# Rotary position exchange by two half-partition copies instead of a matrix product, in a two-block transformer kernel on one core

## The chip, the cores and the metric

The kernel runs on one core of one Trainium2 chip. The metric is the device time of one execution in microseconds (us); lower is better. The core has TensorE (PE, matrix products), VectorE (DVE), ScalarE (ACT), GpSimd (POOL) and the DMA queues; each engine works off its own instructions in order and waits on semaphores.

## What is computed

Two transformer blocks run one after the other on 256 rows of width 1024, all in float32. The first block (conditioned norms, a gated feed-forward, a mixed attention, another feed-forward) has no rotary positions. The second has two layers, and both rotate their queries and keys. Cut to what matters:

```python
def apply_rope(x, cos, sin):                  # x: (B, S, heads, 64), half = 32
    half = x.shape[-1] // 2
    x1, x2 = x[..., :half], x[..., half:]
    return jnp.concatenate([x1 * c - x2 * s, x2 * c + x1 * s], axis=-1)

# layer 1, differential attention: 8 heads, two score maps of 64 dims each
q, k, v = jnp.split(hn @ w_qkv, [1024, 2048], axis=-1)
q = apply_rope(q.reshape(B, S, 16, 64)); k = apply_rope(k.reshape(B, S, 16, 64))
p = softmax(causal(q k^T / 8)); a = p[:, :, 0] - lam * p[:, :, 1]
o = rms_norm(a @ v, subln_g) * (1 - lambda_init); h = h + o @ w_o
h = h + sq_relu_mlp(rms_norm(h))
# layer 2, latent attention: 8 heads, scores over 128 plain + 64 rotated dims
ckv = rms_norm(h) @ w_dkv; c, k_rope = ckv[..., :256], apply_rope(ckv[..., 256:])
q = rms_norm(hn @ w_dq) @ w_uq                # per head 128 plain + 64 rotated
s = (q_nope k_nope^T + apply_rope(q_rope) k_rope^T) * 192**-0.5
h = h + (softmax(causal(s)) @ v) @ w_o; h = h + sq_relu_mlp(rms_norm(h))
return rms_norm(h, final_norm_g)
```

## The kernel before

All weights come through one stream of 1 MB chunks into a ring of five (`raw`); each chunk holds two units of 128x1024. `feed()` splits a unit into a high part (ACT, line 358, `whi`) and the remainder (DVE, line 359, `wlo`), again in a ring of five, and every product of weights is three matmuls (high by high, low by high, high by low: `products`, line 396). Activations are held transposed, features on the 128 partitions and the 256 rows along the free dimension. Small products go through `put` (line 406) and `put_last` (line 409) in plain float32.

PSUM is handed out as a queue of banks (`banks.take`, `banks.give`): four, and four more (`fix`) while they aren't needed as accumulators. A bank that is given back carries the tokens that its next user must wait for. The engines' instructions are emitted in one program order by hand, and the attention heads are threaded into it: a head is a generator (`diff_head`, `latent_head`), and `side.nudge()` advances at most two waiting pieces each time that it is called; a piece names after how many nudges it wants to be continued.

**Layer 1.** For each head `hh`, a q block and a k block of 128 columns are projected (`block_T`, 24 matmuls of 128x256, one nudge in the middle and one behind `feed()`). Each block is then rotated by `roped`. The columns of a block are two heads' halves in their natural order (x1, x2 of one, x1, x2 of the other, 32 partitions each), so the exchange of x1 and x2 is a product with a 128x128 signed permutation, `rotm`:

- ACT copies the block from its bank into `xb` (line 1411, tile `sg`); POOL multiplies it by cosines into `yb` (line 1412, tile `hm`). Here the generator yields.
- At the next nudge, in the middle of the next block (`rope_end`, put in front of the queue by `side.soon`), PE multiplies `xb` by `rotm` into the other half of the bank (line 409), DVE multiplies that by sines (line 1416), gives the bank back, and adds `yb`: one add for k (line 1420), two adds of 64 partitions for q (line 1422), which go into `padded`, where each of the two score maps has its own 128-partition tile with zeros in the other map's half.

A `diff_head` has four pieces: masks, scores, maxima (DVE, line 1153), exponentials (ACT, line 1158) and scaling (DVE, lines 1461 to 1469); the transposes of the probabilities (PE, line 1131; ACT, line 1134); the product with v, the sum of squares (ACT, line 1479), the root by `rstd` (DVE, line 529, then a power on POOL, line 523) and the scaling (DVE, line 1483); the transposes back and the split (PE, line 1490; ACT, line 580; DVE, line 581).

**Layer 2.** One block gives the rotated key `kr`, whose second half of `roped` is called one block of `ukn` later; then `UQ_ORDER` takes for each of four groups one rotated block and two plain ones (`qn`, lines 1642 and 1644). The second half of `roped` is called behind the next plain block's copy. `latent_head` is the head here: scores, exponentials, scaling (DVE, line 1605), then transposes and product with v.

After the loop of each layer `banks.retire(fix)` takes the four accumulator banks out, from the last head's q block in layer 1 and from the third block before the end in layer 2, since the output projection needs them.

Of the kernel before, what the change touches and what calls it, by code (L numbers as in the profile page):

```python
# [7 lines left out]
P = 128  # L8
D = 1024
T = 256  # L10
# [35 lines left out]
for _name, _n in (("ident", 128), ("ones", 128), ("rot", 128), ("tri", 128), ("causal", 128), ("strict", 128), ("flip", 128),  # L46
                  ("cos", 256), ("sin", 256), ("topk", 512), ("bucket", 384)):
    CONST[_name] = (_at, _at + _n)
    _at += _n
# [178 lines left out]
def build(nc, stream, x, c_row, cols, const, g_post, rel, lam, final_g, out):  # L228
    plan = stream_plan()
    with ExitStack() as ctx:  # L230
# [283 lines left out]
        lohi = (slice(0, 64), slice(64, 128))  # L514
        t_zero = t_half
        for c in range(2):
            t_zero = pool.do(lambda e: e.memset(padded[lohi[1 - c], c:24:2, :], 0.0), t_zero)

        def power(r, v, t):
# [3 lines left out]
            return pool.do(lambda e: e.tensor_tensor(r, v, ex, ALU.pow), t, t_zero)  # L523
# [863 lines left out]
        gate_load(2, dve.last(), pe.last())  # L1387
        def other_gates():
            while todo:
                modulations(True)  # L1390
# [13 lines left out]
        cos, sin, rotm = const_of("cos"), const_of("sin"), const_of("rot")  # L1404
        xs = Rooms([Room(sg[:, n, :]) for n in range(2)])
        ys = Rooms([Room(hm[:, n, :]) for n in range(2)])

        def roped(o, b, tk, s):

            xb, yb = xs.take(), ys.take()  # L1410
            t = act.do(lambda e: e.activation(xb.ap, b.ap[:, 0:T], ACT.Copy, scale=s), tk, xb.free)
            t0 = pool.do(lambda e: e.tensor_tensor(yb.ap, xb.ap, cos, ALU.mult), t, yb.free)
            yield
            tk = put_last(b.ap[:, T:2 * T], rotm, xb.ap, True, t)
            turned = o if o.shape[1] == T else xb.ap
            t = dve.do(lambda e: e.tensor_tensor(turned, b.ap[:, T:2 * T], sin, ALU.mult), tk,  # L1416
                       [] if turned is o else t0)
            banks.give(b, t)
            if turned is o:
                t = [dve.do(lambda e: e.tensor_tensor(o, o, yb.ap, ALU.add), t, t0)]  # L1420
            else:
                t = [dve.do(lambda e: e.tensor_tensor(o[q, c, :], xb.ap[q, :], yb.ap[q, :], ALU.add), t, t0)
                     for c, q in enumerate(lohi)]
            xs.give(xb, *t)
            ys.give(yb, *t)
            yield t
# [72 lines left out]
        def rope_end(at, rope):  # L1499
            t_q[at], born[at] = next(rope), side.now  # L1500
            yield

# [302 lines left out]
```

How the kernel before makes its waits and increments, by code:

```python
    def wait(self, *after):  # L116
        for a in after:
            for sem, value in ([a] if isinstance(a, tuple) else a or []):
                if self.seen.get(id(sem), 0) < value:
                    self.seen[id(sem)] = value
                    self.engine.wait_ge(sem, value)
# [1 line left out]
    def do(self, op, *after):  # L124
        self.wait(*after)
        self.count += 1
        op(self.engine).then_inc(self.sem, 1)
        return self.sem, self.count
# [6 lines left out]
    def load(self, out, in_, sem, value, *after):  # L136
        self.wait(*after)
        self.engine.dma_start(out, in_).then_inc(sem, 16)
        return sem, value
```

## Time and profile before

| | |
|---|---|
| median of 3 runs | 1213.88 us (1212.95 to 1217.24) |
| the profiled execution | 1212.7 us |
| its span, first to last instruction | 1211.4 us |
| mean granted TensorE clock | 0.988 |
| PE busy | 1151.8 us (95%), 7570 instructions |
| DVE busy | 808.5 us (67%) |
| ACT busy | 622.6 us (51%) |
| POOL busy | 54.7 us (5%) |

The span is what the trace covers; the execution is 1.3 us longer. The layer-1 blocks with their heads lie at about 617 to 704 us of the span and the layer-2 blocks with theirs at 939 to 1002 us. A busy time is the union of an engine's instructions; matmuls overlap each other in the records, so what one costs is read from the chain, where consecutive starts are shown.

### The profile page before, as it was taken

The page shows a single profiled execution, that of the slowest core. Times are in us where ns is not written, and L with a number is a line of the kernel's source. Part 1 is how long each engine was busy: PE and PEld are TensorE (multiplying, and loading weights), DVE is VectorE, ACT ScalarE, POOL GpSimd, SP SyncE. Part 2 cuts the span into 40 slices and gives each one's busy share as a digit, 9 for nine tenths or more (in the row PEclk, how much of TensorE's full clock was granted, in tenths as well). Part 3 has the DMA queues.
Part 4 walks back from the last instruction along what each step waited for, and adds up shares of the span by engine and source line. Part 5 has one row for each costly group of instructions (what it writes and reads, how often), then busy time and mean ns, then how long its engine had stood idle before and what let it go on. Part 6 is the DMA issues. An engine that isn't in the chain of part 4 may idle for free.

```text
span 1211.4 us, 19269 instructions
## 1 busy us (share of the span) xinstructions
PE 1151.8 (95%) x7570; PEld 1052.6 (87%) x7570; DVE 808.5 (67%) x1334; ACT 622.6 (51%) x1138; POOL 54.7 (5%) x75
## 2 busy tenths in 40 slices
PE   4999999899998999999999898999999889999998
PEld 4988899699987999999799778999998778899997
DVE  4878888777666756555768767565558666656555
ACT  5644444646656544444644455544556444554453
POOL 3100000000001000000012100000000100000000
PEclk9999999999999899999999899999999999999999
DMA  8969998373222566655352234555554413555540
GB/s 345 407 260 411 341 351 308 139 298 118 105 105 71 200 239 211 227 198 176 128 190 100 95 105 150 198 176 195 186 180 153 154 63 102 212 199 177 195 150 35
DMA packets 34009, 231.75 MB, mean 191 GB/s; under 512 B 3704, under 2 KB 5120, under 8 KB 6528
## 3 DMA queue, kind: packets, MB, share of 16 engines
q1 hardware_dynamic: 31952, 226.24, 51.2%
q10 hardware_dynamic: 1968, 4.29, 1.0%
q8 instruction: 60, 0.98, 0.3%
q14 instruction: 29, 0.24, 0.1%
HBM read 229.45 MB, written 1.06 MB: 190 GB/s over the span
## 4 chain that ended last, share of the span: by engine, by line
PE 77%; DVE 11%; ACT 8%; issue 2%; DMA 1%; POOL 1%; DVEq 0%; SPq 0%; ACTq 0%; POOLq 0%
PE ps L396 35%; PE pacc L396 34%; DVE wlo L359 4%; ACT whi L358 2%; PE ps L406 2%; PE ps L409 2%; ACT wk L1158 2%; PE pacc L406 1%; ACT arena L669 1%; POOL st L523 1%; DVE st L1153 1%; DVE tmp L711 1%; DMA raw<-in_stream 1%; DMA cst<-in_const 1%; PE pacc L409 1%
## 5 line engine op out<-in xcount | busy, mean ns | idle before, releaser
L359 DVE TENSOR_TENSOR wlo<-raw,whi 128x1024 fp32r<-128x1024 f32 x353 | 430.2, 1225 | 177.1 <-ACT whi L358 168.7
L358 ACT ACTIVATE whi<-raw 128x1024 fp32r<-128x1024 f32 x353 | 368.8, 1055 | 163.1 <-PE pacc L396 83.2
L396 PE MATMUL ps<-nhi,whi 128*128 128x256 f32 x1256 | 362.7, 289 | 2.6 <-DVE arena L1416 1.1
L396 PE MATMUL ps<-nlo,whi 128*128 128x256 f32 x1256 | 357.0, 284 | 0.0
L396 PE MATMUL ps<-nhi,wlo 128*128 128x256 f32 x1256 | 356.9, 284 | 0.0
L396 PEld LDWEIGHTS ps<-nhi,whi 128*128 128x128 f32 x1256 | 242.4, 193 | 8.5 <-DVE arena L1416 1.4
L396 PEld LDWEIGHTS ps<-nlo,whi 128*128 128x128 f32 x1256 | 242.4, 193 | 4.4 <-issue 0.5
L396 PEld LDWEIGHTS ps<-nhi,wlo 128*128 128x128 f32 x1256 | 242.3, 193 | 0.0
L879 ACT ACTIVATE sg<-ps 128x256 f32<-128x256 f32 x104 | 39.9, 384 | 165.2 <-PE ps L396 165.2
L396 PE MATMUL pacc<-whi,mhi 128*128 128x512 f32 x240 | 95.6, 398 | 0.0
L396 PE MATMUL pacc<-wlo,mhi 128*128 128x512 f32 x240 | 94.0, 392 | 0.0
L396 PE MATMUL pacc<-whi,mlo 128*128 128x512 f32 x240 | 93.5, 390 | 0.0
L881 DVE TENSOR_TENSOR hm<-sg,ps 128x256 f32<-128x256 f32 x104 | 43.6, 420 | 69.8 <-ACT sg L879 69.8
L336 DVE SCALAR_TENSOR_TENSOR raw<-raw,silu_c 128x1024 f32<-128x1024 f32 x72 | 87.6, 1225 | 0.0
L396 PE MATMUL pacc<-whi,hhi 128*128 128x512 f32 x188 | 74.1, 394 | 3.9 <-DVE hlo L888 3.2
L396 PE MATMUL pacc<-wlo,hhi 128*128 128x512 f32 x188 | 73.6, 391 | 0.0
L396 PE MATMUL pacc<-whi,hlo 128*128 128x512 f32 x188 | 73.2, 389 | 0.0
L523 POOL TENSOR_TENSOR st<-st,mod 128x1 f32<-128x1 f32 (+1 forms) x40 | 24.9, 623 | 1006.6 <-DVE st L674 801.6
L396 PE MATMUL pacc<-whi,nhi 128*128 128x512 f32 (+1 forms) x128 | 50.8, 397 | 7.4 <-DVE nlo L750 3.8
L396 PEld LDWEIGHTS pacc<-whi,mlo 128*128 128x128 f32 x240 | 45.1, 188 | 9.9
L396 PEld LDWEIGHTS pacc<-whi,mhi 128*128 128x128 f32 x240 | 45.3, 189 | 8.2 <-issue 0.5
L396 PEld LDWEIGHTS pacc<-wlo,mhi 128*128 128x128 f32 x240 | 45.3, 189 | 7.7 <-issue 0.5
(316 smaller groups left out, 1783.3 us busy)
## 6 DMA issues: line engine op xcount, KB each, us to landing
raw<-in_stream SPq DMA_DIRECT2D x213, 1024.0 KB, 4.9
gates<-in_g_post ACTq DMA_DIRECT2D x3, 512.0 KB, 7.4
h<-in_x SPq DMA_DIRECT2D x1, 1024.0 KB, 7.2
cst<-in_const ACTq DMA_DIRECT2D x1, 1024.0 KB, 4.8
arena<-bias_rows ACTq DMA_DIRECT2D x1, 1024.0 KB, 14.4
out<-tmp SPq DMA_DIRECT2D x4, 256.0 KB, 2.2
silu_c<-in_c_row ACTq DMA_DIRECT2D x1, 512.0 KB, 5.8
arena<-in_final_g SPq DMA_DIRECT2D x1, 512.0 KB, 3.8
```

The lines of the kernel that those rows point to most:

```text
L336: t = dve.do(lambda e: e.scalar_tensor_tensor(src, src, 1.0, silu_c[:, :], ALU.mult, ALU.mult, accum_out=adac[:, 8 * m + k:8 * m + k + 1]) ...
L358: t_hi = act.do(lambda e: e.activation(whi[:, s, :], src, ACT.Copy), arrived, room)
L359: t_lo = dve.do(lambda e: e.tensor_tensor(wlo[:, s, :], src, whi[:, s, :].bitcast(F32), ALU.subtract), arrived, room, t_hi)
L396: return e.matmul(o, lt[a], rh[b], start=start and first, stop=stop and last)
L406: pe.quiet(lambda e: e.matmul(o, lt, rh, start=start, stop=stop), *after)
L409: return pe.do(lambda e: e.matmul(o, lt, rh, start=start, stop=True), *after)
L523: return pool.do(lambda e: e.tensor_tensor(r, v, ex, ALU.pow), t, t_zero)
L669: return act.do(lambda e: e.activation(junk, src, ACT.Square, scale=D ** -0.5, accum_out=sums[:, f:f + 1]), *after)
L711: t = dve.do(lambda e: e.tensor_scalar(tmp[:, i, w], h[:, i, w], r, None, ALU.mult), t, self.new[i])
L879: t = act.do(lambda e: e.activation(sg[:, m, :], up if gate is None else gate, ACT.Relu if gate is None else ACT.Silu), tk)
L881: t = dve.do(lambda e: e.tensor_tensor(hm[:, m, :], sg[:, m, :], up, ALU.mult), t)
L1158: toks.append(act.do(lambda e: e.activation(dst.ap[:, a:a + w], src[:, a:a + w], ACT.Exp, bias=mx[:, i:i + 1], accum_out=sm[:, i:i + 1]), ...
```

## The change

The q and k projection columns (and the rotated columns of layer 2) are laid out on the host with both heads' first halves ahead of both heads' second halves, so that the exchange of x1 and x2 is an exchange of the upper and the lower 64 partitions. ACT does it while it copies out of PSUM, POOL multiplies by signed sines, and the matrix `rotm` and its product are gone. The two score maps' parts are then four stripes of 32 partitions, two for each map, so q is written by four adds, and two more memsets give the zeros that this needs. `roped` is no longer a generator: all of it is emitted right behind the block, ahead of `feed()`. The bank is given back with the ACT copies' token.

```diff
-for ... (("ident", 128), ("ones", 128), ("rot", 128), ("tri", 128), ...
+for ... (("ident", 128), ("ones", 128), ("tri", 128), ...
...
+        quads = [slice(32 * n, 32 * n + 32) for n in range(4)]
...
+        zeroed = [t_zero]
...
-            return pool.do(lambda e: e.tensor_tensor(r, v, ex, ALU.pow), t, t_zero)
+            return pool.do(lambda e: e.tensor_tensor(r, v, ex, ALU.pow), t, zeroed[-1])
...
         cross.finish(20)
         gate_load(2, dve.last(), pe.last())
+        t_quads = pe.last()
+        for n, q in enumerate(quads[1:3]):
+            t_quads = pool.do(lambda e: e.memset(padded[q, n:16:2, :], 0.0), t_quads)
+            zeroed.append(t_quads)
...
-        cos, sin, rotm = const_of("cos"), const_of("sin"), const_of("rot")
+        cos, sin = const_of("cos"), const_of("sin")
         xs = Rooms([Room(sg[:, n, :]) for n in range(2)])
         ys = Rooms([Room(hm[:, n, :]) for n in range(2)])
+        turned = sb("turned", [P, 2, T])
+        rs_ = Rooms([Room(turned[:, n, :]) for n in range(2)])
 
         def roped(o, b, tk, s):
 
-            xb, yb = xs.take(), ys.take()
+            xb, yb, xr = xs.take(), ys.take(), rs_.take()
             t = act.do(lambda e: e.activation(xb.ap, b.ap[:, 0:T], ACT.Copy, scale=s), tk, xb.free)
+            for to, of in (lohi, lohi[::-1]):
+                t1 = act.do(lambda e: e.activation(xr.ap[to, :], b.ap[of, 0:T], ACT.Copy, scale=s), tk, xr.free)
+            banks.give(b, t1)
             t0 = pool.do(lambda e: e.tensor_tensor(yb.ap, xb.ap, cos, ALU.mult), t, yb.free)
-            yield
-            tk = put_last(b.ap[:, T:2 * T], rotm, xb.ap, True, t)
-            turned = o if o.shape[1] == T else xb.ap
-            t = dve.do(lambda e: e.tensor_tensor(turned, b.ap[:, T:2 * T], sin, ALU.mult), tk,
-                       [] if turned is o else t0)
-            banks.give(b, t)
-            if turned is o:
-                t = [dve.do(lambda e: e.tensor_tensor(o, o, yb.ap, ALU.add), t, t0)]
+            t1 = pool.do(lambda e: e.tensor_tensor(xr.ap, xr.ap, sin, ALU.mult), t1)
+            if o.shape[1] == T:
+                t = [dve.do(lambda e: e.tensor_tensor(o, xr.ap, yb.ap, ALU.add), t0, t1)]
             else:
-                t = [dve.do(lambda e: e.tensor_tensor(o[q, c, :], xb.ap[q, :], yb.ap[q, :], ALU.add), t, t0)
-                     for c, q in enumerate(lohi)]
-            xs.give(xb, *t)
+                t = [dve.do(lambda e: e.tensor_tensor(o[q, n % 2, :], xr.ap[q, :], yb.ap[q, :], ALU.add), t0, t1, t_quads)
+                     for n, q in enumerate(quads)]
+            xs.give(xb, t0)
             ys.give(yb, *t)
-            yield t
+            rs_.give(xr, *t)
+            return t
...
-                rope = roped(kT[:, hh, :] if g else qT[:, 2 * hh:2 * hh + 2, :], b, tk, 1.0 if g else 0.125)
-                next(rope)
+                t = roped(kT[:, hh, :] if g else qT[:, 2 * hh:2 * hh + 2, :], b, tk, 1.0 if g else 0.125)
                 feed()
                 side.nudge()
-                side.soon(rope_end(g + hh, rope))
+                t_q[g + hh], born[g + hh] = t, side.now + 1
...
-        rope = roped(kr, b, tk, 1.0)
-        next(rope)
+        t_kr = roped(kr, b, tk, 1.0)
...
-                if n == 1:
-                    t_kr = next(rope)
...
-                if pend is not None:
-                    t_qr[pend[0]], born[pend[0]] = next(pend[1]), side.now
-                    pend = None
             else:
-                rope = roped(qr[:, 2 * (blk - 8):2 * (blk - 8) + 2, :], b, tk, scale)
-                next(rope)
-                pend = (blk - 8, rope)
+                t_qr[blk - 8] = roped(qr[:, 2 * (blk - 8):2 * (blk - 8) + 2, :], b, tk, scale)
+                born[blk - 8] = side.now + 1
...
-    put("sin", np.sin(ang).astype(np.float32).T[i % 32])
+    put("sin", np.where(i[:, None] < 64, -1.0, 1.0) * np.sin(ang).astype(np.float32).T[i % 32])
...
+def halves_first(w):
+
+    k, m = w.shape
+    return w.reshape(k, m // P, 2, 2, 32).transpose(0, 1, 3, 2, 4).reshape(k, m)
...
-    src["qk"] = tiles_T(w[:, 0:2048])
+    src["qk"] = tiles_T(halves_first(w[:, 0:2048]))
```

The columns of `dkr` and the rotated part of `uq` go through `halves_first` in the same way.

## Rows read from the trace of the kernel before

**Rows 1.** The page: PE's busy time, and the chain's shares by engine.
```profile
PE 1151.8 (95%) x7570; PEld 1052.6 (87%) x7570; DVE 808.5 (67%) x1334; ACT 622.6 (51%) x1138; POOL 54.7 (5%) x75
...
PE 77%; DVE 11%; ACT 8%; issue 2%; DMA 1%; POOL 1%; DVEq 0%; SPq 0%; ACTq 0%; POOLq 0%
```

**Rows 2.** Busy time in stretches: PE, PEld, DVE, ACT, POOL, granted clock, DMA.
```profile
657.65:668.62 10.97, 9.99 (x73) 9.26 (x74) 8.76 (x23) 5.53 (x18) 2.16 (x3) 1.00 0.28 97
...
691.00:692.00 1.00, 1.00 (x5) 1.00 (x6) 1.00 (x2) 0.00 (x0) 0.00 (x0) 0.50 0.00 0
```

**Rows 3.** The chain in order of time, first layer-1 blocks: start, length, what.
```profile
625.77 2.87 PE ps L396 x24
628.63 0.43 PE ps L409 x2
```

**Rows 4.** Single lines: ns shortest/median/longest, first and last start.
```profile
L1412 POOL TENSOR_TENSOR hm<-sg,cst x21: 727/755/1015, 621.8 to 986.4; 128x256 f32<-128x256 f32 x21
...
L1422 DVE TENSOR_TENSOR arena<-sg,hm x24: 416/422/856, 624.4 to 990.2; 64x256 f32<-64x256 f32 x24
...
L1114 ACT ACTIVATE arena<-ps x7: 362/377/379, 262.3 to 335.7; 64x256 f32<-64x256 f32 x7
```

**Rows 5.** Timeline of DVE, layer 1: start, length, instruction, [idle before <-releaser].
```profile
633.11 1.15 DVE L1153 TENSOR_REDUCE st<-pacc 128x1 f32<-128x128 f32 x4
...
666.54 0.76 DVE L1467 TENSOR_SCALAR wk<-wk,st 128x128 f32<-128x128 f32 x1
...
668.39 0.42 DVE L1416 TENSOR_TENSOR arena<-pacc,cst 128x256 f32<-128x256 f32 x1
668.84 0.42 DVE L1420 TENSOR_TENSOR arena<-arena,hm 128x256 f32<-128x256 f32 x1
669.19 1.22 DVE L359 TENSOR_TENSOR wlo<-raw,whi 128x1024 fp32r<-128x1024 f32 x1
...
671.68 0.61 DVE L1483 TENSOR_SCALAR wk<-pacc,st 128x128 f32<-128x128 f32 x2 [0.80 <-POOL st L523]
...
672.65 0.87 DVE L1422 TENSOR_TENSOR arena<-sg,hm 64x256 f32<-64x256 f32 x2
...
674.70 1.14 DVE L1153 TENSOR_REDUCE st<-ps 128x1 f32<-128x128 f32 x4
676.36 0.17 DVE L1461 RECIPROCAL st<-st 128x2 f32<-128x2 f32 x1 [0.52 <-ACT wk L1158]
...
698.48 1.15 DVE L1153 TENSOR_REDUCE st<-ps 128x1 f32<-128x128 f32 x4
...
701.29 0.28 DVE L1467 TENSOR_SCALAR wk<-wk,st 128x128 f32<-128x128 f32 x1
```

**Rows 6.** Timeline of POOL: the first block's end, and layer 1.
```profile
584.84 0.55 POOL L523 TENSOR_TENSOR st<-st,mod 128x1 f32<-128x1 f32 x1 [191.79 <-DVE st L674]
...
666.45 0.77 POOL L1412 TENSOR_TENSOR hm<-sg,cst 128x256 f32<-128x256 f32 x1 [5.08 <-ACT sg L1411]
670.95 0.69 POOL L523 TENSOR_TENSOR st<-st,mod 128x2 f32<-128x2 f32 x1 [3.74 <-DVE st L529]
671.60 0.74 POOL L1412 TENSOR_TENSOR hm<-sg,cst 128x256 f32<-128x256 f32 x1
```

**Rows 7.** Timeline of DVE, layer 2, third group and the next head.
```profile
975.69 1.02 DVE L1605 TENSOR_SCALAR wk<-wk,st 128x128 f32<-128x128 f32 x2
977.10 1.23 DVE L359 TENSOR_TENSOR wlo<-raw,whi 128x1024 fp32r<-128x1024 f32 x1 [0.38 <-PE ps L1131]
978.24 0.42 DVE L1644 TENSOR_SCALAR arena<-ps 128x256 f32<-128x256 f32 x1
...
982.84 0.68 DVE L1605 TENSOR_SCALAR wk<-wk,st 128x128 f32<-128x128 f32 x2
```

**Rows 8.** Timeline of PE, layer 2, two of its waits.
```profile
942.89 0.39 PE L396 MATMUL ps<-hhi,whi 128*128 128x256 f32 x1 [1.61 <-DVE arena L1268]
...
980.03 0.46 PE L406 MATMUL pacc<-arena 128*128 128x128 f32 x2 [0.40 <-DVE arena L1422]
```

More of the change, by code:

```diff
@@ L45 @@
 _at = 0
-for _name, _n in (("ident", 128), ("ones", 128), ("rot", 128), ("tri", 128), ("causal", 128), ("strict", 128), ("flip", 128),
+for _name, _n in (("ident", 128), ("ones", 128), ("tri", 128), ("causal", 128), ("strict", 128), ("flip", 128),
                   ("cos", 256), ("sin", 256), ("topk", 512), ("bucket", 384)):
@@ L1497, in build @@
             side.add(diff_head(hh), lambda hh=hh: ripe(hh, 8 + hh))
-        def rope_end(at, rope):
-            t_q[at], born[at] = next(rope), side.now
-            yield
         for hh in range(8):
@@ L1621, in build @@
             side.add(latent_head(hh), lambda hh=hh: hh in t_qn and ripe(8 + hh, hh // 2))
-        units, pend = [], None
+        units = []
         for n, blk in enumerate(UQ_ORDER):
@@ L1679, in constants @@
     put("ident", np.eye(P))
-    r = np.zeros((P, P))
-    for m in range(P):
-        if m % 64 < 32:
-            r[m + 32, m] = -1.0
-        else:
-            r[m - 32, m] = 1.0
-    put("rot", r)
     put("flip", np.eye(P)[::-1])
@@ L1739, in lay_out @@
     src["dkv"] = w[:, 0:256].reshape(2, 4, P, 256).transpose(0, 2, 1, 3).reshape(2, P, 1024)
-    src["dkr"] = tiles_T(np.concatenate([w[:, 256:320], w[:, 256:320]], axis=1))
+    src["dkr"] = tiles_T(halves_first(np.concatenate([w[:, 256:320], w[:, 256:320]], axis=1)))
     w = v["w_ukv_2"].reshape(256, 8, 256)
@@ L1746, in lay_out @@
     w = v["w_uq_2"][0].reshape(384, 8, 192)
-    w = np.concatenate([w[:, :, 0:128].reshape(384, 1024), w[:, :, 128:192].reshape(384, 512)], axis=1)
+    w = np.concatenate([w[:, :, 0:128].reshape(384, 1024), halves_first(w[:, :, 128:192].reshape(384, 512))], axis=1)
     w = tiles_T(w)[UQ_ORDER].transpose(1, 0, 2).reshape(P, 36 * P)
```

## The prediction

> **What bounds the kernel now.** I read the page first. PE is busy for 95% of the span and has 77% of the chain [rows 1], so a change that takes matmuls away looks like a gain of as much. The chain in order of time puts a number on it: in the first layer-1 blocks a rotation stands between two runs of matmuls with 0.43 us, beside 2.87 us for a block's 24 matmuls [rows 3]. There are 21 rotations [rows 4], so PE gives up 21 x 0.43 = 9.0 us. That is a gain only where PE sets the pace, and the timeline of DVE says that around the rotations it mostly doesn't.
>
> From the first head's maxima (633.11) on, DVE is idle only in named waits: for POOL's power (0.80 us in each head) and for the exponentials (0.52 us, and a like wait for the second score map) [rows 5]. Everything else stands back to back until the bank queue is cut, ahead of the seventh head's maxima (698.48). In the steady part a head takes 10.97 us, and PE has 9.99 us of records in it [rows 2], in which it waits for ACT's copy, which stands behind the exponentials. So the pace from the third to the sixth head is DVE's, its work plus three short waits, and PE follows with about 1 us to spare in each head. DVE's turn, in order: scaling of the probabilities; product and add of a k block (668.39, 668.84); a split (669.19); the head's third piece, behind POOL (671.68); product and two adds of a q block (672.65); a split; the maxima (674.70) [rows 5].
>
> Layer 2 is a chain through all engines. PE waits 0.40 us for the q add at 980.03 [rows 8], and that add stands behind the scaling, a split and the plain copy on DVE [rows 7].
>
> **The change, part by part.**
>
> *DVE's work.* A k block loses its product, 668.39 to 668.84, 0.45 us, and keeps one add. A q block loses the same and gets four adds for two, and two take 0.87 [rows 5]. The trace has no 32-partition add, but adds over 64 partitions and over 128 both take 0.42 us for 256 columns [rows 4, 5], so a stripe counts the same: +0.87 - 0.45 = +0.42. For a head that is -0.45 + 0.42 = 0.0. (Bounds: nothing or +0.87 for the two extra adds, so -0.9 to 0 a head; the equal widths speak for the upper.) DVE's turn isn't made shorter.
>
> *Order.* The rotation takes no nudge slots any more, so I count a head's pieces half a block (1.43 us) earlier, each in the middle of a block. DVE's sequence stays as above. Ahead of the first head PE has three rotations and their first wait less, and by hand it reaches the first scores some 3 us earlier. DVE, which has to take the first adds behind POOL, comes to its first maxima at about 630.8 in place of 633.1: **-2.3 us**. This head start is all that PE's savings buy before DVE has the pace.
>
> *New wait, q blocks.* DVE's adds now need POOL's second product. POOL does the power (670.95), then the cosines (671.60 to 672.34) [rows 6], then the sines, until 673.0 to 673.1. DVE is done with its third piece at 672.20. So it waits some **0.85 us**, and queued behind it on DVE are the adds, the next split and the maxima, for which ACT's exponentials wait. From the third head on each turn has this. (Bounds: 0, if ACT's copies and POOL came before the power, which the order forbids; 1.4, with both products at their slowest, 1.015 us [rows 4].)
>
> *New contention, k blocks.* POOL's cosines start behind the first copy, and with the sines it now works for 1.5 us, all of it while DVE scales probabilities for 2.3 us. So the k add waits for nothing. But the scaling suffers: L1467 takes 0.76 us beside POOL's product (666.54 on DVE, 666.45 on POOL) and 0.28 us with POOL idle (701.29) [rows 5, 6]. One product costs DVE 0.5 us. What a second costs no row shows; bounds 0 and its whole 0.74 us. I take **0.6 us**, nearer to the upper, since its neighbour cost nearly that.
>
> The Trainium skill's page "SBUF — State Buffer" (section "Who interferes with whom") says that GpSimd and VectorE share a port pair as an exclusive lock, that a VectorE instruction with two SBUF inputs takes it as well, and that the loser waits for the whole instruction. By that rule a turn loses 0.74 us and layer 1 comes out 0.7 us later than I say; by a price of 0 it is 3 us earlier.
>
> *Layer 1, the sum.* The start gives -2.3. The turn to the second head has only the contention, +0.6; the four turns to the sixth have both, 4 x 1.45 = +5.8, together +4.1. The turn to the seventh was 12.8 us before (PE stood at a bank; its start at 698.48 [rows 5]) and is a common turn now, 10.97 + 1.45 = 12.4: +3.7. The last key's add moves with it and gates the last head, behind which PE works with 0.3 us of slack: **+3.4 us** (bounds -2.3 with neither wait, +6.5 with both at their upper ends).
>
> *ACT and the banks.* 42 more copies of 64 partitions, 0.38 us each [rows 4], 16 us at most on an engine busy for half of the turn [rows 2]. They lie beside DVE's scaling and PE's next matmuls; without that cover a block's last wait grows by 0.75. The bank comes free with the copies and no longer with DVE's product, which is worth something only at the cut of the queue, counted above.
>
> *Layer 2, four q blocks.* The adds now stand ahead of the split and of the plain copy, and the next head's scores need all of them. Third group before: scaling done at 976.71, a wait of 0.38, split (977.10), copy (978.24) [rows 7], product, adds until 979.9. Now: scaling done at 976.7, or at 977.3 if the sines hold it up as the cosines did (1.02 for the pair of L1605 against 0.68 [rows 7]); adds from 977.3 for 1.74 us, split 1.14, copy 0.33: 980.5. The adds are no longer last, the plain copy is, 1.9 us later than at 978.57, and all scores wait for it: 1.1 us at their end. By the same count the first two groups lose 0.8 and 0.65: **+3.0 us**, less what PE's shorter stretch gives back, 0.6 in all (bounds +1 and +5).
>
> *Layer 2, the key.* PE already waits 1.61 us for a DVE copy at 942.89 [rows 8]. Now DVE's add waits for two products that are queued behind two powers, and the split and that copy come 1.3 us later; the bank that is free earlier lets PE do one block (0.7) more ahead of it: **+0.5 us** (0 to 1.3).
>
> *Nothing:* the two new memsets, 2048 columns each. At POOL's 0.76 us for 256 columns they take 6 us each at most, in 192 us in which POOL has nothing (ahead of 584.84 [rows 6]); right ahead of that power they would cost it all. The constant load is 64 KB smaller and nothing waits for it.
>
> *Sum:* 3.4 + 2.4 to 3.0 + 0.5, with 3.0 kept: **+6.9 us** on the profiled 1212.7 (the span of 1211.4 and 1.3 around it), 1219.6. The median of the runs is 1.2 us above that execution; I say 1220.
>
> **Rivals.**
>
> *Faster: PE's time counts.* If the waits for POOL didn't show and a stripe's add cost half, DVE's turn would fall to about 10.5 us, the head start would grow to the end of the layer, and PE's 9.0 us would come back nearly whole: 1204 to 1207. For it speaks PE's 95% [rows 1]. Against it: DVE's timeline without gaps, and adds that take the same time over 64 and 128 partitions. It decides once DVE's turn is under PE's own 9.5 us.
>
> *Nearly nothing.* The second product doesn't hold DVE's scaling up, and only the wait behind the power is new: layer 1 +0.4, layer 2 +1.5, key +0.3: about 1215. For it: L1483 beside a product at full speed (671.68, 0.61 for two [rows 5]).
>
> *The clock.* PE now runs ahead and then stands for up to 3 us in each turn. Before, it stood like that near 686, and at 691 five matmuls took 1 us at a granted clock of 0.50, which is the 1.2 GHz level [rows 2], against 0.12 us each in a block [rows 3]: half a block costs 1.5 us more. In the turns PE has room for that; if the drops last, or fall where a stage ends, four or five of them add 6 to 8 us: 1227.
>
> **Chances and range.** Forecast (1217 to 1224) 0.50; nearly nothing (1212 to 1217) 0.23; faster 0.12; clock 0.15. A change of 0.5%, 6.1 us, is about what a measurement of this kernel can tell from none. Slower than 1219.9: 0.3 out of the forecast's half and all of the clock's, 0.45. Faster than 1207.8: 0.12. Within: 0.43. The range for 8 in 10 is 1211 to 1227; the forecast's own is 1217 to 1224.
>
> **What would show it.** PE busy some 9 us less and idle for longer in the heads' turns. In layer 1 DVE idle for 0.6 to 1 us ahead of the first of four adds, released by POOL; L1467 at over 1 us; heads 12.4 us apart instead of 10.97. In layer 2 the plain copy behind the adds, and PE waiting for it. The prediction is wrong if heads stand at 11 us or less, if DVE has gaps in which it waits for PE, or if a stripe's add takes half of 0.42 us.

## The result and the profile after

The changed kernel takes 1231.49 us (median of 4 runs, 1228.96 to 1231.72) beside 1213.61 for the kernel before in the same session: 17.9 us slower. The ratio over all runs is 1.0138 [1.0126, 1.015], which is 16.7 us. I had said 1220, and 1227 as the upper end. The profiled execution of the changed kernel is its fastest run, 1228.96, so what is read from its profile explains about 16 us, and the last 1 to 2 us of the median are placed nowhere. PE did get 21 products less (two instructions each), and POOL's time rose with 21 products more:

```profile
PE 1147.4 (93%) x7528; PEld 1049.8 (86%) x7528; DVE 819.9 (67%) x1337; ACT 639.9 (52%) x1180; POOL 74.1 (6%) x98
...
PE 70%; DVE 15%; ACT 8%; issue 3%; POOL 2%; DMA 1%; DVEq 0%; SPq 0%; ACTq 0%; POOLq 0%
```

PE's busy time fell by 4.4 us only, where 9 were expected: in e7 below, with as many PE instructions, it is 1139.7 us, and here part of the matmuls runs at a lower granted clock. Against [rows 1] PE's share of the chain fell from 77 to 70%, and DVE's rose from 11 to 15%. Where the time went is read from landmarks that both kernels have: POOL's powers at the norms and DVE's maxima of each head. From the power at 584.84 [rows 6] (585.82 now) to the norm behind layer 1's output projection (727.50 before, 736.45 now) the change costs 7.97 us; the feed-forward behind it costs nothing; from the next power (914.13, 923.08) to the one behind layer 2's output projection (1019.02, 1035.27) it costs 7.30. About 1 us lies ahead of all changed work; that first power stands between 583.74 and 588.27 in the profiles of this document.

**Layer 1, the turns.** DVE in the fifth head's turn, changed kernel (start, length, instruction, idle before and its releaser), to be read against [rows 5]:

```profile
671.39 0.77 DVE L1475 TENSOR_SCALAR wk<-wk,st 128x128 f32<-128x128 f32 x1
672.19 0.79 DVE L1477 SCALAR_TENSOR_TENSOR wk<-wk,st 128x128 f32<-128x128 f32 x1
...
676.51 0.61 DVE L1491 TENSOR_SCALAR wk<-pacc,st 128x128 f32<-128x128 f32 x2 [0.80 <-POOL st L526]
677.98 1.76 DVE L1429 TENSOR_TENSOR arena<-turned,hm 32x256 f32<-32x256 f32 x4 [0.86 <-POOL turned L1425]
679.77 1.23 DVE L359 TENSOR_TENSOR wlo<-raw,whi 128x1024 fp32r<-128x1024 f32 x1
680.91 1.14 DVE L1156 TENSOR_REDUCE st<-ps 128x1 f32<-128x128 f32 x4
```

POOL in the same stretch:

```profile
671.30 0.77 POOL L1424 TENSOR_TENSOR hm<-sg,cst 128x256 f32<-128x256 f32 x1 [5.75 <-ACT sg L1420]
672.11 0.73 POOL L1425 TENSOR_TENSOR turned<-turned,cst 128x256 f32<-128x256 f32 x1
...
676.44 0.74 POOL L1424 TENSOR_TENSOR hm<-sg,cst 128x256 f32<-128x256 f32 x1
677.13 0.74 POOL L1425 TENSOR_TENSOR turned<-turned,cst 128x256 f32<-128x256 f32 x1
```

Maxima stand at 668.58 and 680.91, a turn of 12.33 us where it was 10.97. Two things are new: the wait of 0.86 us ahead of the four adds, released by the sines, and L1477 beside the sines of the k block, 0.79 us where its twin before took 0.35. The windows from maxima to maxima (busy PE, PEld, DVE, ACT, POOL, clock, DMA) say the same: DVE busy 9.27 for 8.76 [rows 2], 0.5 us more, and with the wait that is the whole 1.36.

```profile
668.58:680.91 12.33, 10.47 (x86) 10.19 (x85) 9.27 (x23) 7.16 (x22) 3.59 (x5) 1.00 0.26 86
680.91:693.22 12.31, 8.78 (x47) 8.25 (x46) 9.28 (x24) 7.16 (x22) 3.55 (x5) 0.72 0.25 85
```

In the second of these turns the granted clock is 0.72, and the turn is no longer for it: PE has room.

**Layer 1, the first blocks**, where I had counted a gain. DVE again:

```profile
624.46 2.63 DVE L1429 TENSOR_TENSOR arena<-turned,hm 32x256 f32<-32x256 f32 x4 [1.41 <-POOL turned L1425]
627.12 1.23 DVE L359 TENSOR_TENSOR wlo<-raw,whi 128x1024 fp32r<-128x1024 f32 x1
628.27 0.95 DVE L1427 TENSOR_TENSOR arena<-turned,hm 128x256 f32<-128x256 f32 x1
629.14 1.74 DVE L359 TENSOR_TENSOR wlo<-raw,whi 128x1024 fp32r<-128x1024 f32 x1
...
633.74 1.14 DVE L1156 TENSOR_REDUCE st<-pacc 128x1 f32<-128x128 f32 x4
```

and POOL beside it:

```profile
624.97 0.95 POOL L1424 TENSOR_TENSOR hm<-sg,cst 128x256 f32<-128x256 f32 x1 [0.61 <-ACT sg L1420]
625.89 0.92 POOL L1425 TENSOR_TENSOR turned<-turned,cst 128x256 f32<-128x256 f32 x1
627.42 1.51 POOL L1424 TENSOR_TENSOR hm<-sg,cst 128x256 f32<-128x256 f32 x1 [0.62 <-ACT sg L1420]
```

An operation that reads two operands from SBUF on DVE and meets a product on POOL is held up: four adds take 2.63 for 1.76, the k add 0.95 for 0.42, the split at 629.14 takes 1.74 for 1.22. Here the later one of the two pays: the split at 627.12 was running when POOL began at 627.42, keeps its 1.23, and there the product takes 1.51 for 0.74.

**Layer 2.** PE at the scores of the first head, of one in the second group and of one in the fourth, changed kernel:

```profile
968.77 2.08 PE L406 MATMUL ps<-arena 128*128 128x128 f32 x6 [3.34 <-DVE arena L1644]
970.64 1.06 PE L409 MATMUL ps<-arena 128*128 128x256 f32 x2
...
981.10 1.14 PE L406 MATMUL ps<-arena 128*128 128x128 f32 x6 [0.81 <-DVE arena L1644]
982.08 0.60 PE L409 MATMUL ps<-arena 128*128 128x256 f32 x2
...
1005.32 0.44 PE L406 MATMUL ps<-causalr,identr 128*128 128x384 f32 x1 [2.13 <-DVE arena L1644]
1005.60 1.19 PE L406 MATMUL ps<-arena 128*128 128x128 f32 x6
1006.57 1.06 PE L409 MATMUL ps<-arena 128*128 128x256 f32 x2
```

and the granted clock (next to last but two) around them:

```profile
965.00:969.00 4.00, 0.66 (x5) 0.40 (x4) 3.44 (x8) 1.63 (x3) 1.32 (x2) 0.98 0.30 127
969.00:972.00 3.00, 3.00 (x11) 2.64 (x12) 1.23 (x3) 0.00 (x0) 0.00 (x0) 0.50 0.18 35
...
1007.00:1010.00 3.00, 3.00 (x11) 2.60 (x10) 1.21 (x5) 1.67 (x5) 0.00 (x0) 0.54 0.00 0
```

PE waits 3.34 us for the plain copy, which is now last (before, it waited 0.40 for the adds in such a place [rows 8]), and then works at half the clock, the 1.2 GHz level: the scores take 2.9 us from 968.77, where the same eight matmuls take 1.6 us at full clock (from 981.10). The second drop comes some 1 us behind a wait of 2.13. So the length of the wait is not the whole price.

### The profile page after: what moved, and what is told of

It is laid out like the page before. It is cut to its first block, busy times and chain, and to the rows that moved or that the text cites. A ratio compares the mean times of both kernels' runs of the same rounds, so it can differ in the third digit from the quotient of the medians.

```text
span 1227.6 us, 19279 instructions
## 1 busy us (share of the span) xinstructions
PE 1147.4 (93%) x7528; PEld 1049.8 (86%) x7528; DVE 819.9 (67%) x1337; ACT 639.9 (52%) x1180; POOL 74.1 (6%) x98
## 4 chain that ended last, share of the span: by engine, by line
PE 70%; DVE 15%; ACT 8%; issue 3%; POOL 2%; DMA 1%; DVEq 0%; SPq 0%; ACTq 0%; POOLq 0%
PE ps L396 33%; PE pacc L396 31%; DVE wlo L359 5%; ACT whi L358 2%; PE ps L406 2%; ACT wk L1161 2%; DVE arena L1429 2%; PE pacc L406 1%; POOL st L526 1%; ACT arena L672 1%; PE ps L409 1%; DVE st L1156 1%; DVE tmp L714 1%; DMA cst<-in_const 1%; DMA raw<-in_stream 1%
## 5 line engine op out<-in xcount | busy, mean ns | idle before, releaser
L359 DVE TENSOR_TENSOR wlo<-raw,whi 128x1024 fp32r<-128x1024 f32 x353 | 431.8, 1230 | 170.4 <-ACT whi L358 164.0
```

Source lines behind the costliest of these rows:

```text
L359: t_lo = dve.do(lambda e: e.tensor_tensor(wlo[:, s, :], src, whi[:, s, :].bitcast(F32), ALU.subtract), arrived, room, t_hi)
```

## The experiments

Layer 1 and layer 2 are the two distances between powers named above, against 142.66 and 104.89 us before; the turn is the distance of maxima in the middle of layer 1 (between the third head and the sixth: one turn, or their range). All from one profiled execution of each, which isn't always near the median: it is 1228.96 for the changed kernel, 1214.33 for e2 and 1211.69 for e12. The kernel before had medians of 1213.28 to 1214.38 in the sessions, so a saving beside the changed kernel that is given in us, as a difference of medians, comes out up to 1 us smaller by the ratios.

| kernel | median us | ratio to before | layer 1 | layer 2 | turn |
|---|---|---|---|---|---|
| changed | 1231.49 | 1.0138 [1.0126, 1.015] | +8.0 | +7.3 | 12.33 |
| e1 late adds | 1224.74 | 1.0087 [1.0072, 1.0102] | +6.2 | +4.3 | 11.83 |
| e2 no sines | 1216.51 | 1.0022 [1.0012, 1.0032] | -0.9 | +2.5 | 11.1 to 11.2 |
| e3 sines on DVE | 1226.72 | 1.0108 [1.0091, 1.0125] | +6.5 | +6.7 | 12.0 to 12.1 |
| e4 two adds | 1219.51 | 1.0046 [1.0031, 1.0061] | +1.2 | +5.8 | 11.44 |
| e5 before, copies | 1219.08 | 1.0044 [1.0031, 1.0057] | +3.4 | +3.7 | 10.96 to 11.05 |
| e6 before, POOL | 1221.04 | 1.0056 [1.0037, 1.0074] | +6.8 | +0.8 | 11.6 to 11.9 |
| e7 before, no rotation | 1212.74 | 0.9988 [0.9975, 1.0001] | -1.0 | +0.2 | 11.0 to 11.1 |
| e8 sums on PE | 1218.28 | 1.0031 [1.0021, 1.0041] | -0.2 | +5.4 | 10.35 |
| e9 no copies | 1229.62 | 1.0124 [1.0108, 1.014] | +8.5 | +6.7 | 12.2 to 12.5 |
| e10 stripes by ACT | 1242.65 | 1.0242 [1.0227, 1.0257] | +22.8 | +6.8 | 14.17 |
| e11 one add | 1227.63 | 1.0111 [1.0098, 1.0124] | +13.6 | +0.2 | 12.98 |
| e12 sums on PE, later | 1215.4 | 1.0005 [0.9994, 1.0016] | +0.1 | +0.1 | 10.3 to 10.6 |
| e13 layer 1 only | 1221.29 | 1.0063 [1.0049, 1.0078] | +7.9 | 0 | 12.31 |
| e14 layer 2 only | 1222.11 | 1.0069 [1.0055, 1.0084] | +0.5 | +8.1 | 11.0 |
| e15 no sines, two adds | 1209.42 | 0.9955 [0.9938, 0.9971] | -5.8 | +1.5 | 10.33 |
| e16 late, two adds | 1214.78 | 1.0018 [1.0006, 1.003] | -0.1 | +1.0 | 10.92 |
| e17 four ACT copies | 1223.71 | 1.0081 [1.0067, 1.0095] | +4.6 | +4.5 | 11.04 |

**e1_late_adds.** The second half of `roped`, DVE's adds, is emitted where it was before.

```diff
+            xs.give(xb, t0)
+            yield
             if o.shape[1] == T:
...
-                t_q[g + hh], born[g + hh] = t, side.now + 1
+                side.soon(rope_end(g + hh, rope))
```

> The kernel after, with its copies, its POOL products and its four narrow adds, but the adds are emitted where the kernel before had its second half (at the nudge in the middle of the next block; in layer 2 behind the next plain copy). Placement theory: what costs is that the adds stand in DVE's queue before POOL can be ready and ahead of the split and the plain copy; then DVE's 0.84 us waits ahead of the adds (5 of them in layer 1) and most of layer 2's 7.3 us go, and the time is 1214 to 1219. Contention theory: what costs is POOL's second product running beside DVE (1.33 us more in each turn, of which 0.44 in the scaling); that stays, and the time stays at 1225 to 1231. Work theory: DVE's adds cost what the products saved, order doesn't matter: 1228 to 1231.

6.7 us come back of 17.9 (6.2 by the ratios). The wait is gone, but not its cause. DVE, this kernel:

```profile
677.61 0.61 DVE L1492 TENSOR_SCALAR wk<-ps,st 128x128 f32<-128x128 f32 x2 [0.80 <-POOL st L526]
678.14 2.20 DVE L1431 TENSOR_TENSOR arena<-turned,hm 32x256 f32<-32x256 f32 x4
```

The add now belongs to the block before, so nobody waits; it lies beside the next block's product on POOL instead, and takes 2.20 for 1.76. A wait was turned into a hold-up.

**e2_no_sines** and **e3_sines_on_dve.**

```diff
-            t1 = pool.do(lambda e: e.tensor_tensor(xr.ap, xr.ap, sin, ALU.mult), t1)
+            t1 = dve.do(lambda e: e.tensor_tensor(xr.ap, xr.ap, sin, ALU.mult), t1)      (e3; e2 has no such line)
```

> The kernel after without POOL's multiplication by the sines (the exchanged halves are added unscaled; that part of the computation is left out). Contention and placement theories both lose here: the wait of 0.84 us goes in 5 turns (4.2 us) and the scaling gets 0.44 us back in 7 turns (3 us), layer 2 gets back 0.7 us in 4 groups and perhaps the drop of the clock (2 us): 1219 to 1223. If the work of DVE is what costs, nothing changes: 1229 to 1231.

> The kernel after with the multiplication by the sines on DVE instead of POOL (same computation). POOL theory: DVE works 0.43 us longer in each of 21 blocks (9 us) but waits 0.85 less in the turns with the power in front and isn't held up by a second product; in a steady turn that is +0.87 - 0.85 - 0.44 = -0.4: about 1227 to 1230, hardly any change. Work theory: DVE's own work is all that counts, +0.87 us in each of 8 turns and +0.43 in 4 groups: 1238 to 1241.

One product more of 0.74 us a block, on an engine that is busy for 6% of the span, costs 15 us (14 by the ratios). DVE in e2 has the scaling at its old length and no wait:

```profile
666.38 0.35 DVE L1476 SCALAR_TENSOR_TENSOR wk<-wk,st 128x128 f32<-128x128 f32 x1
...
670.95 1.76 DVE L1428 TENSOR_TENSOR arena<-turned,hm 32x256 f32<-32x256 f32 x4
```

and the head start is there: the first maxima stand at 631.19, where I had put them (630.8). On DVE the same product costs 10 of these 15 us (0.42 us and a gap of 0.1 behind it, for two blocks of a head).

**e4_two_adds.** Two adds of 64 partitions in place of four of 32.

```diff
-                t = [dve.do(lambda e: e.tensor_tensor(o[q, n % 2, :], ...
-                     for n, q in enumerate(quads)]
+                t = [dve.do(lambda e: e.tensor_tensor(o[q, c, :], ...
+                     for c, q in enumerate(lohi)]
```

> The kernel after with q written by two adds of 64 partitions instead of four of 32 (parts of q then lie in the other score map's tile, so that the scores are other ones). Work theory: 0.88 us less of DVE in each of 12 q blocks, 10.5 us: 1219 to 1221, the steady turn from 12.33 to 11.45 us. If the waits for POOL set the turn and a shorter add only lengthens them, under 5 us: 1226 to 1229.

12 us (11 by the ratios) come back. The adds take 0.87 us for 1.76, so a turn is 0.89 us shorter (11.44 for 12.33): a narrow add costs as much as a wide one, as predicted, and on an engine that sets the pace there is nothing that hides it.

**e5_before_copies** and **e6_before_pool** put one suspect each into the kernel before.

```diff
+            (e5) for to, of in (lohi, lohi[::-1]):
+                dead[0] = act.do(lambda e: e.activation(spare[to, dead[1], :], cos[of, :], ACT.Copy, scale=s), dead[0])
+            (e6) dead[0] = pool.do(lambda e: e.tensor_tensor(spare[:, dead[1], :], cos, sin, ALU.mult), dead[0])
```

> The kernel before with two more ACT copies over 64 partitions behind each of the 21 block copies (of the cosine table, into a spare tile that nobody reads). Cover theory: ACT has room in layer 1 but stands ahead of the rotation there, where PE waits for ACT (0.9 us a turn): 0.5 us more in some blocks of PE's wait, but DVE's turn stays at 10.97; 1214 to 1218. ACT theory (the copies are what makes the kernel after slow): 0.5 us or more in each of 21 blocks, 1224 or more.

> The kernel before with a second 128x256 product on POOL behind each cosine product (cosine table by sine table into a spare tile; nobody waits for it). Contention theory: no wait is added, but DVE is held up beside it: 0.44 us in the scaling of each of 7 turns and as much for the q block's product or adds, so the turn goes from 10.97 to 11.8 and the time to 1219 to 1224. If contention is small and only the waits count, the time stays within 2 us of before.

In e6 nobody waits for the product, and it still costs layer 1 6.8 us, 2.0 of them in the turn to the seventh head, where PE stands at a bank. DVE's turn has one more hold-up for each of the two products more:

```profile
671.04 0.80 DVE L1466 TENSOR_SCALAR st<-st 128x2 f32<-128x2 f32 x1
671.76 0.84 DVE L1470 TENSOR_SCALAR wk<-wk,st 128x128 f32<-128x128 f32 x1
...
677.95 1.12 DVE L1425 TENSOR_TENSOR arena<-sg,hm 64x256 f32<-64x256 f32 x2
```

The scaling of the sums takes 0.80 where a turn before has 0.23, and the two adds 1.12 for 0.87. In e5 the common turns don't move, but the turn to the seventh head takes 14.9 us for 12.8, and PE's clock in it is

```profile
690.00:697.00 7.00, 5.47 (x23) 5.30 (x24) 5.34 (x13) 1.80 (x6) 0.69 (x1) 0.51 0.09 36
```

and in the same stretch of the kernel before it is 0.71 with PE busy for 6.12 us. Here nobody reads the copies, and they still cost 4.7 us by the medians. In the profile, whose two distances add up to 7.1, that turn is 2.1 us. The larger part, 3.7 us, lies in layer 2: in its third and fourth group DVE waits 1.18 and 1.21 us for ACT's high part ahead of a split, where it waits 0.38 and 0.41 us in the kernel before, for PE.

**e7_before_no_rotation.** The kernel before without its 21 products with `rotm`.

```diff
-            tk = put_last(b.ap[:, T:2 * T], rotm, xb.ap, True, t)
+            tk = t
...
-            ... e.tensor_tensor(turned, b.ap[:, T:2 * T], sin, ALU.mult), tk,
+            ... e.tensor_tensor(turned, b.ap[:, 0:T], sin, ALU.mult), tk,
```

> The kernel before without the 21 matrix products of the rotation: DVE multiplies the unrotated block in the bank by the sines (the exchange of the halves is left out). It gives the price of what the change takes from PE. DVE theory: DVE sets the pace in layer 1 and keeps all its work, so that of 9.0 us only the part from the blocks ahead of the first heads and the drained end comes back: 1210 to 1213. PE theory: most of the 9 us, 1204 to 1206.

PE's 9.0 us, the first thing that one sees in the page, are worth 1.6 us, and the interval reaches to none. The turn stays at 10.96 to 11.07, since DVE's doesn't need PE.

**e8_pe_sums** and **e12_pe_sums_later** take all of DVE's work out of the rotation: POOL makes both products, PE adds them up in PSUM (`rotm` times one, the identity times the other), ACT copies out. In e12 only in layer 1 and one block later.

```diff
+            put(b.ap[:, T:2 * T], rotm, zb.ap, True, False, t, t1)
+            tk = put_last(b.ap[:, T:2 * T], ident, yb.ap, False, t0)
```

> The kernel before (natural column layout) with the rotation's sum on PE: POOL makes x times sine and x times cosine, PE adds rotm by the one and the unit matrix by the other in PSUM, ACT copies the sum out (one copy for k, two for q); DVE has no part in it. Same computation. DVE loses 2.15 us of work a turn and gains 0.44 to 0.9 of contention, PE gets 0.43 us more in each block. If DVE's turn is what binds, the turn falls from 10.97 to about PE's 9.5 + 0.9 = 10.4 us and the time to 1207 to 1213; if PE or the longer way over POOL binds, 1214 to 1222.

> PE sums the two POOL products in PSUM, as before, but in layer 1 only and one whole block later, so that PE doesn't wait for POOL in the first blocks; layer 2 as in the kernel before. With DVE's turn at about 9.3 us PE's own 10.4 binds; 5 turns x 0.6 us and a first head that isn't late: 1208 to 1212. If the bank held for one block more stops PE where the four accumulator banks are taken out, 1214 to 1218.

e8's turn, 10.35 us, is PE's: it is busy for 10.00 of the 10 us from 664, and its first maxima are 3.4 us late: the two products of a rotation take PE 1.24 us in the first blocks, where one took 0.43, with a wait of 0.32 for POOL's second product in each (on the weight load), and PE stands once for 1.07 us ahead of the first. In e12 the waits come back on DVE, which now waits for ACT and PE, and its split stays beside POOL's products:

```profile
664.26 1.22 DVE L359 TENSOR_TENSOR wlo<-raw,whi 128x1024 fp32r<-128x1024 f32 x1 [0.53 <-ACT whi L358]
...
668.60 1.52 DVE L359 TENSOR_TENSOR wlo<-raw,whi 128x1024 fp32r<-128x1024 f32 x1 [1.08 <-PE pacc L1131]
```

Nothing that a measurement can tell from the kernel before is won.

**e9_after_no_copies.** The changed kernel without ACT's 42 exchange copies; POOL multiplies the block as it is.

```diff
-            for to, of in (lohi, lohi[::-1]):
-                t1 = act.do(lambda e: e.activation(xr.ap[to, :], b.ap[of, 0:T], ACT.Copy, scale=s), tk, xr.free)
...
-            t1 = pool.do(lambda e: e.tensor_tensor(xr.ap, xr.ap, sin, ALU.mult), t1)
+            t1 = pool.do(lambda e: e.tensor_tensor(xr.ap, xb.ap, sin, ALU.mult), t, xr.free)
```

> The kernel after without the 42 exchange copies on ACT: POOL multiplies the unexchanged block by the sines (the exchange is left out); POOL's products, the early place and the four adds stay. If the copies cost as much here as in the kernel before (4.7 us there, most of it in layer 2), the time falls to 1226 to 1228. If they lie beside POOL and DVE here, 1230 to 1232; if everything new hangs on ACT, under 1222.

The ratio is 0.0014 below the changed kernel's, 1.7 us, and the intervals overlap. The 4.7 us of e5 are not found here. One part of them, the turn in which PE stood at a bank, is a common turn in this kernel; why layer 2 gets no more than 0.6 us back was not followed.

**e10_stripes_by_act** (changed kernel, late adds) and **e11_one_add** (kernel before, layer 1): DVE adds once for all 128 partitions, ACT copies the parts to their tiles.

```diff
+                t = dve.do(lambda e: e.tensor_tensor(yb.ap, xr.ap, yb.ap, ALU.add), t0, t1)
+                t = [act.do(lambda e: e.activation(o[q, n % 2, :], yb.ap[q, :], ACT.Copy), t, t_quads)
+                     for n, q in enumerate(quads)]
```

> The late-adds kernel with one DVE add of 128 partitions for a q block and four ACT copies of 32 partitions into the stripes. DVE's turn loses 1.3 us (11.83 to about 10.5), ACT's grows by about 1.1. DVE theory: 12 blocks x 1.3 are some 10 us in layer 1 and a few in layer 2, less the price of the copies: 1215 to 1219. If ACT binds once it has four more instructions, 1221 or more.

> The kernel before with, in layer 1 only, one add of 128 partitions for a q block and two ACT copies into the halves, in place of two adds. DVE theory: 0.45 us less in each turn, 10.97 to 10.5, five or six binding turns: 2 to 3 us, 1211 to 1213. If the turn hangs on PE and ACT as much as on DVE, no change.

Both were to be faster. e10 is the slowest of all, and e11 is 13 us slower than the kernel before. DVE's work did shrink, by three adds in e10 and one in e11; what it got is a gap. ACT and then DVE in e10:

```profile
674.31 1.73 ACT L1432 ACTIVATE arena<-hm 32x256 f32<-32x256 f32 x4 [3.50 <-DVE hm L1431]
```

```profile
673.86 0.42 DVE L1431 TENSOR_TENSOR hm<-turned,hm 128x256 f32<-128x256 f32 x1
678.44 1.23 DVE L359 TENSOR_TENSOR wlo<-raw,whi 128x1024 fp32r<-128x1024 f32 x1 [4.16 <-ACT whi L358]
```

ACT stands for 3.5 us behind DVE's add with the copy of the next block and the next unit's high part queued behind it, and then DVE stands 4.2 us for that high part. Two engines that were side by side work in turn. e11 has the same: ACT stands for 4.92 us behind DVE's add (695.89), and DVE then 2.48 us for the high part (698.33).

**e13_layer1_only** and **e14_layer2_only**: the change in one layer, the kernel before in the other.

```diff
+        def roped_n(o, b, tk, s):       # the changed roped; called in one of the layers
+            for (to, of), g in ((lohi, -s), (lohi[::-1], s)):
+                t1 = act.do(lambda e: e.activation(xr.ap[to, :], b.ap[of, 0:T], ACT.Copy, scale=g), tk, xr.free)
```

> The change in layer 1 alone: layer 2 keeps the matrix product and the old column layout, and the signs of the sines come from the scale of ACT's copies, so that both layers use one table. Theory (each layer has its own loss): layer 1 loses 8 us as in the changed kernel and layer 2 nothing, 1222 to 1223, with the first power behind the second feed-forward of layer 1 some 8 us later than before and all distances behind it as before. Rival (what layer 1 does shifts layer 2's waits or its clock): layer 2 is longer by 2 us or more although nothing in it is changed, 1225.

> The change in layer 2 alone (its key and its four q blocks; 5 rotations of 21); the two memsets go behind layer 1's output projection. Theory: layer 2 loses 7.3 us as in the changed kernel, 1221 to 1222. Rival: half of layer 2's loss comes from where layer 1 leaves the stream and the clock, and alone it loses what I predicted, 3 to 3.5 us: 1217 to 1218.

+8.0 and +8.8 us against the 1213.28 of that session, together 16.8 of 17.9: the layers' losses are their own (by the ratios 1.0063 and 1.0069 of 1.0138). (In e13 some of the zero stripes of layer 2 keep layer 1's values; no instruction is more or less for it.) Layer 2 with its 5 rotations loses as much as layer 1 with 16.

**e15_no_sines_two_adds** and **e16_late_two_adds** combine.

```diff
-            t1 = pool.do(lambda e: e.tensor_tensor(xr.ap, xr.ap, sin, ALU.mult), t1)      (e15 alone)
-                     for n, q in enumerate(quads)]                                        (both)
+                     for c, q in enumerate(lohi)]
```

> The changed kernel without POOL's sine product and with two adds of 64 partitions in place of four of 32 (the products with the sines are left out, and the parts of q stand in the wrong stripes). Theory A (two prices, paid one behind the other on DVE): they add up until PE's own work bounds a head, at about 9.5 to 9.8 us of turn: layer 1 is 8 to 9 us shorter than before and the kernel takes 1205 to 1207. Theory B (both are paid in the same wait): no better than with the larger one alone, 1214 to 1216. In between would be the floor that some other wait sets: the power on POOL and the exponentials leave DVE idle for about 2 us in each turn whatever its work is, and the turn comes to 10.3, 1209.

> The changed kernel with the adds emitted where they stood before and two of them in place of four (the parts of q stand in the wrong stripes). The sines stay. Theory A: the two savings, 6.7 and 12 us, belong to different terms and add up: 1212 to 1214, a turn near 10.9. Theory B: emitted late, the two adds lie beside POOL's sines and take 1.1 to 1.3 in place of 0.87, and the scaling stays held up: turn 11.1 to 11.3, 1216 to 1218. If it is under 1212, the late place alone with cheap stripes would beat the kernel before.

In the turn the two prices add up: 12.33 less some 1.16 (e2) less 0.89 (e4) is 10.28, and e15 has 10.33. Of the whole time 22 us come back, not the 27 (25 by the ratios) of e2 and e4 together, for 1209, the value that I had given for a turn of 10.3 with DVE's short waits left in it (0.80 us for the power, 0.52 and 0.64 for exponentials; all three are in its trace). At 0.45% faster it is the only one that differs from before in that direction, and it leaves out the sines. e16 is 10 us faster than e1 (8 by the ratios) and ends between the two theories: the two adds take 1.28 us beside POOL's product and the scaling is still held up, as B has it, and the turn is 10.92, as A has it.

**e17_four_act_copies** is the whole computation with e16's order: natural column order, ACT exchanges in four copies of 32 partitions, DVE needs two adds.

```diff
+            for n in range(4):
+                t1 = act.do(lambda e: e.activation(xr.ap[quads[n], :], b.ap[quads[n ^ 1], 0:T], ACT.Copy,
+                                                   scale=s if n % 2 else -s), tk, xr.free)
```

> The whole computation: the exchange stays with ACT and the sines with POOL, but the projection columns keep their natural order, so ACT exchanges in four copies of 32 partitions (84 in place of 42, the signs in their scale) and DVE needs two adds for q; the adds stand where they stood before the change. Theory (ACT has room, and DVE's narrow pieces were the cost): as the run with late adds and two of them, 1214 to 1216, at most 2 us above it for ACT's longer copies, so 1214 to 1218. Rival (ACT's copies are late for POOL's sines, which then run beside more of DVE's work, and hold up ACT's part of the split): 1220 to 1224, no better than the changed kernel with late adds.

The rival was right. The turn stays at 11.04, as the theory wants. But ACT's four copies take twice the time of two, POOL waits for them,

```profile
672.32 1.57 ACT L1422 ACTIVATE turned<-ps 32x256 f32<-32x256 f32 x4
```

```profile
673.96 0.73 POOL L1426 TENSOR_TENSOR turned<-turned,cst 128x256 f32<-128x256 f32 x1 [0.87 <-ACT turned L1422]
```

and the time goes outside the common turns. Counted from the power ahead, its first maxima stand 1.4 us later than e16's (50.1, 48.7): DVE waits there 2.48 and 1.02 us for ACT's high part, 1.69 us and not at all in e16. The turn to the third head costs 1.4 more and the last one 1.2, and layer 2 has +4.5 for +1.0; which waits carry it there was not followed further. No whole version that was run beats the kernel before.

## Why the prediction was wrong

**Right.** What sets the pace: DVE, with PE's 9 us hidden (e7). The narrow adds at the price of wide ones (1.76 for four; e4). The wait behind the power (0.85 said, 0.86 seen) and the hold-up of the scaling (0.6 said, 0.44 seen, in L1477 and not in L1467, where I had expected it): a turn of 12.4 said, 12.33 seen. The turn to the seventh head (-0.4 said, -0.5 seen), and layer 1's common four (+5.8 said, +5.4 seen). The key: +0.5 said, nothing seen; the copies at 955.85 before stand 41.7 us behind the power in both kernels.

**Wrong, layer 1 (+3.4 said, +8.0 seen).** The step that failed is the one that begins "DVE comes to its first maxima at about 630.8". I took the two products on POOL as a cost only where DVE scales, and in the first blocks as nothing. There both products lie beside DVE's adds and split, and the two engines hold each other up: -0.35 us in place of -2.3. e2, where the product is out, has the start that I had counted. The same is behind the turn to the second head, +1.5 for +0.6: k add 0.95, split 1.75. And the last turn, for which I had no term, costs +1.6 (9.60 for 7.99): before, its scaling ran with POOL idle (0.28 at 701.29 [rows 5]), now it has both products beside it (0.76 and 0.81: +0.94), and one split more lies in it (+1.1), less DVE's own product (-0.45). These three make 4.5 of the 4.6 us by which layer 1 is off; the other terms' errors (-0.5 and +0.6) cancel.

**Wrong, layer 2 (+3.0 said, +7.3 seen).** The mechanism was right, the plain copy behind the adds, and its size was not. Group by group, from maxima to maxima: +2.9, +0.5, +1.4, +1.9, and +0.5 for the last head. I had 0.8 in the first, gave the fourth no figure of its own (0.45 is left for it in the 3.0), and had no term for a fall of the clock behind a wait: the eight matmuls behind it take 1.35 us more (2.93 for 1.58) at the granted clock of 0.50, and in the fourth group 0.45 (2.03 for 1.58), with 0.7 more for the product with v behind it, of which the last head's distance shows 0.5: 2.3 to 2.5 us together. My rival of the clock named this ("or fall where a stage ends") at a chance of 0.15, but put it into layer 1's turns, where it cost nothing. The rest, about 5 us, is the order with its wait of 0.69 for the sines in two groups: e1 undoes the order alone and gives 3.0 us back, e2 the sines and gives 4.8; both include the clock where the wait shrinks (in e1 PE stands in two pieces, 1.05 and 1.00 us, at the first scores, and they run at full clock). How far each of them does is left open.

The Trainium skill's page "SBUF — State Buffer" (section "Who interferes with whom") says that GpSimd and VectorE lock a port pair against each other, that a VectorE instruction with two SBUF inputs contends for it too, and that whoever comes first keeps it for its whole instruction while the other blocks. The trace agrees: L1427 takes 0.95 for 0.42, L359 1.74 for 1.22, and POOL 1.51 for 0.74 beside a split that began before it. I had read the price as a whole product, 0.74 us. In the pairs read here it is what is left of the other's instruction, less 0.1 to 0.2 us: L1427 begins 0.66 us ahead of the product's end and is held for 0.53, L1477 0.65 and 0.44, POOL's product 0.93 ahead of the split's end and 0.77. Applied to every such pair, and not to the scaling alone, the rule would have shown me the first blocks.

**The sum itself.** 1219.6 and the 1.2 us by which the median lies above the profiled execution make 1220.8, and I said 1220; the 0.8 us decide nothing.

## What to carry to other kernels

Ask of a change that takes work from the busiest engine which engine works without gaps where the change acts: taking PE's products away was by itself worth 1.6 of 9 us (0 to 3 by its interval), and what was put on DVE or beside it counted in full. A product on an idle POOL is not free: look which SBUF operations of DVE lie beside it, in the first and last blocks of a stage too, and count a hold-up of some 0.4 to 0.5 us for each product of this size. Before an instruction goes to an engine with room, look what is queued behind it there: e10 and e11 took adds from DVE and made their kernels 18 and 13 us slower, because the next high part stood on ACT behind a wait for DVE.

## What the runs showed of the hardware

- The hold-up works both ways and is not seen in busy shares: POOL's product of 128x256 takes 0.74 us alone and up to 1.51 beside DVE. In the pairs above the one that begins later is held, for what is left of the other, less 0.1 to 0.2 us; with starts 0.05 us apart it was DVE, the earlier one (671.04 in e6, POOL at 671.09). It hits adds, the split and `SCALAR_TENSOR_TENSOR`, and also a small `TENSOR_SCALAR` on SBUF if that is what DVE has when a product starts (0.80 for 0.23 in e6). L1491, which reads PSUM, keeps its 0.61 for two.
- 256 columns take DVE 0.42 us over 128, 64 or 32 partitions (median 417 ns over 48 adds of 32), and ACT 0.38 us over 64 and over 32 (1.57 for four, L1422 in e17).
- After PE stood for 3.34 us its next matmuls ran at half the clock (2.08 us for six that take 1.14), and after 2.13 us those that began some 1 us later, in both cases for about 3 us. e14 repeats the first (3.33 us, then 2.08). In a turn that DVE sets, a clock of 0.72 over 12.3 us cost nothing.
